# Gathering an MoE layer's tokens to partitions 32 to 95, with 28 of 64 experts on 64 slots

## What is computed

```python
scores = jax.nn.sigmoid(xf @ w_router)                  # 520 x 64
...
_, idx = lax.top_k(jnp.where(emask, biased, -jnp.inf), TOP_K)   # 8 of 64 experts per token
gates = w_sel / jnp.sum(w_sel, axis=-1, keepdims=True) * ROUTED_SCALE
...
hb = jax.nn.silu(xb @ w1_e[e]) * (xb @ w3_e[e])         # xb: the tokens of expert e
return (hb @ w2_e[e]) * g[:, None]
```

## Time and profile before

| | |
|---|---|
| median of three runs | 1209.22 us |
| the profiled execution's own time | 1210.91 us |
| its span, first to last instruction | 1209.1 us |
| PE / DVE / ACT / POOL, busy share of the span | 93% / 35% / 21% / 15% |
| mean granted TensorE clock | 0.98 of full speed |
| HBM read and written | 300.15 and 29.36 MB |
| gathers, and their issue on POOL | 64, about 0.98 us each |
| scatters, and their issue on POOL | 64, 1.01 to 1.13 us each |

### The profile page before, as it was taken

The page is one execution under the profiler, slowest core; times in us unless marked ns, Lnnn a source line. Parts: engine busy times, 40 slices in busy tenths (PEclk is TensorE's granted clock), DMA queues, the critical chain, the costliest instruction groups (busy, mean ns, idle before and its releaser), DMA issues.

```text
span 1209.1 us, 21090 instructions
## 1 busy us (share of the span) xinstructions
PE 1124.7 (93%) x8298; PEld 751.8 (62%) x8298; DVE 421.4 (35%) x1046; ACT 258.0 (21%) x566; POOL 176.2 (15%) x210
## 2 busy tenths in 40 slices
PE   7999997999988898999999999999999999999963
PEld 6888644877865687777655556555555555555410
DVE  0359998132058425741111212121121212112034
ACT  1101234022041125101122222222222222222200
POOL 3120050000000000112222222122221222212100
PEclk9999998999999999999999999999999999999978
DMA  9630404034047353358999999999999999999496
GB/s 331 239 140 1 157 13 174 1 140 157 1 140 272 146 211 146 125 186 307 350 385 386 374 386 389 387 388 389 387 381 381 384 387 390 385 383 373 152 379 256
DMA packets 66313, 319.16 MB, mean 264 GB/s; under 512 B 10311, under 2 KB 16671, under 8 KB 39629
## 3 DMA queue, kind: packets, MB, share of 16 engines
q1 hardware_dynamic: 51269, 278.60, 60.2%
q0 software_dynamic: 13568, 35.48, 8.6%
q10 hardware_dynamic: 1424, 4.35, 0.9%
HBM read 300.15 MB, written 29.36 MB: 273 GB/s over the span
## 4 chain that ended last, share of the span: by engine, by line
PE 67%; DVE 16%; DMA 13%; ACT 2%; issue 1%; SPq 1%; DVEq 0%; POOLq 0%
PE psum L755 60%; DMA arena<-in_w_e_dram 8%; DVE act_mem L1717 7%; PE psum L770 6%; DMA arena<-y_rows 3%; DVE mk_mem L1879 2%; DMA arena<-in_w_in_dram 1%; SPq L546 1%; DVE act_mem L1935 0%; ACT act_mem L1500 0%; DVE act_mem L2084 0%; DVE act_mem L1814 0%; ACT act_mem L1509 0%; DVE act_mem L1731 0%; DVE act_mem L2095 0%
## 5 line engine op out<-in xcount | busy, mean ns | idle before, releaser
L755 PE MATMUL psum<-arena,act_mem 128*32 128x128 f32 (+6 forms) x4800 | 509.1, 361 | 9.1 <-DMA arena<-in_w_e_dram 7.9
L755 PEld LDWEIGHTS psum<-arena,act_mem 128*32 128x32 f32 (+5 forms) x4800 | 260.6, 123 | 196.7 <-issue 107.5
L755 PE MATMUL psum<-act_mem,arena 128*128 128x260 f32 (+1 forms) x1728 | 357.7, 369 | 7.1 <-DMA arena<-in_w_o_dram 1.3
L755 PEld LDWEIGHTS psum<-act_mem,arena 128*128 128x128 f32 x1728 | 309.7, 195 | 52.6 <-DMA arena<-in_w_in_dram 2.4
L770 PE MATMUL psum<-ident,act_mem 96*128 96x96 f32 (+8 forms) x484 | 79.5, 296 | 16.5 <-DVE act_mem L1818 6.8
L678 POOL DMA_INDIRECT y_rows<-act_mem,idx_y x40 | 45.1, 1128 | 315.3 <-DVE idx_x L2116 169.8
L2128 DVE TENSOR_SCALAR act_mem<-psum,act_mem 96x512 f32<-96x512 f32 (+1 forms) x40 | 29.9, 747 | 157.7 <-PE psum L755 157.7
L1717 DVE SCALAR_TENSOR_TENSOR act_mem<-act_mem,wcb 128x511 f32<-128x511 f32 (+29 forms) x120 | 77.8, 735 | 0.0
L770 PEld LDWEIGHTS psum<-ident,act_mem 96*128 96x128 f32 (+8 forms) x484 | 59.1, 178 | 28.7 <-issue 12.3
L2125 DVE TENSOR_TENSOR act_mem<-act_mem,psum 128x192 f32<-128x192 f32 x35 | 12.4, 354 | 175.6 <-ACT act_mem L1573 175.6
L755 PEld LDWEIGHTS psum<-act_mem 128*96 128x96 bf16 (+4 forms) x379 | 27.0, 121 | 50.0 <-issue 49.3
(11 more groups left out here) (268 smaller groups left out, 717.6 us busy)
## 6 DMA issues: line engine op xcount, KB each, us to landing
arena<-in_w_e_dram SPq DMA_DIRECT2D x192, 1024.0 KB, 12.9
arena<-y_rows SPq DMA_DIRECT2D x8, 2048.0 KB, 23.9
arena<-in_w_in_dram SPq DMA_DIRECT2D x16, 512.0 KB, 18.1
arena<-in_cache_mem_k_dram SPq DMA_DIRECT2D x8, 1024.0 KB, 8.4
arena<-in_cache_mem_v_dram SPq DMA_DIRECT2D x8, 1024.0 KB, 11.8
arena<-in_w_v_dram SPq DMA_DIRECT2D x1, 4096.0 KB, 24.7
arena<-in_w_k_dram SPq DMA_DIRECT2D x1, 4096.0 KB, 13.8
arena<-in_w_out_dram SPq DMA_DIRECT2D x1, 4096.0 KB, 13.8
```

The source lines that it names most:

```text
L755: return pe.matmul(out, lhsT, rhs, start=first, stop=last)
```

## The change

There are 28 light positions instead of 24, in a period of 16. Apart from the big experts, tokens are gathered to partitions from 32 on: 32 to 95 for the first 64 tokens, 96 to 127 for what a heavy expert has beyond. These tokens beyond 64 have a gather and a scatter of their own (for big experts too), with semaphores `m_gm` and `m_sm` and row numbers `more_x` and `more_y`. PE transposes all 128 partitions for light and heavy experts alike, and ACT copies out the columns of the slots in use, in one instruction. The constants of POOL become 46 instead of 29.

```diff
+ROWS_AT = 32
-NB = 8
-LIGHT = (2, 5, 7)
-HEAVY = (0, 1, 3, 4, 6)
+NB = 16
+BIGS = 8
+LIGHT = (2, 4, 6, 9, 11, 13, 15)
+HEAVY = (0, 1, 3, 5, 7, 8, 10, 12, 14)
...
-SORT_CONSTS = 13 + 2 * NB
+SORT_CONSTS = 14 + 2 * NB
...
+def like(k, mod):
+
+    return [h for h in HEAVY if h % mod == k % mod]
+
+
+def halves_out(i, k, mod):
+
+    hs = like(k, mod)
+    return len(hs) * (i + k // NB) + sum(1 for h in hs if h <= k % NB)
...
-            number(slots_m.rearrange("p (e j) -> p e j", e=LANES), [[1, LANES], [LANES, MCAP // LANES]], 1)
+            number(slots_m[:, 0:LCAP].rearrange("p (e j) -> p e j", e=LANES), [[1, LANES], [LANES, LCAP // LANES]], 1)
+            number(slots_m[:, LCAP:MCAP].rearrange("p (e j) -> p e j", e=LANES), [[1, LANES], [LANES, MORE // LANES]], LCAP + 1)
...
-            def gather(n, b, s, cap=CAP):
+            def gather(n, b, s, cap=CAP, at=0, idx=idx_x):
                 gp.indirect_dma_start(
-                    out=xg[b][0:cap, :], out_offset=None, in_=x2_rows[:, :],
-                    in_offset=bass.IndirectOffsetOnAxis(ap=idx_x[0:cap, n:n + 1], axis=0),
+                    out=xg[b][at:at + cap, :], out_offset=None, in_=x2_rows[:, :],
+                    in_offset=bass.IndirectOffsetOnAxis(ap=idx[0:cap, n:n + 1], axis=0),
...
-                gather(n, n % 4, m_g[n % 4], LCAP if is_light(n) else CAP if is_big(e) else MCAP)
+                at = 0 if is_big(e) else ROWS_AT
+                gather(n, n % 4, m_g[n % 4], LCAP, at)
+                if not is_light(n):
+                    gather(n, n % 4, m_gm[n % 4], CAP - LCAP if is_big(e) else MORE, at + LCAP, more_x)
...
-                    scatter(n, n % 2, m_s[n % 2], CAP if is_big(e) else MCAP)
+                    scatter(n, n % 2, m_s[n % 2], LCAP)
+                    scatter(n, n % 2, m_sm[n % 2], CAP - LCAP if is_big(e) else MORE, LCAP, more_y)
...
-            def turn_few(n):
+            def turn_all(n):
                 for k in range(KC):
-                    last = turn(psum[:, 1, LCAP * k:LCAP * k + LCAP], xg[n % 4][0:LCAP, k:D:KC], LCAP)
+                    last = turn(psum[:, 1, P * k:P * k + P], xg[n % 4][:, k:D:KC])
                 return last
...
+            def b_step(e, k, i):
+                n = k % NB
+                pe.wait_ge(m_g[n % 4], 16 * (NB // 4 * i + (k // 4 + 1)))
+                if not is_light(n):
+                    pe.wait_ge(m_gm[n % 4], 16 * halves_out(i, k, 4))
                 if at_least(e, 1):
                     pe.wait_ge(m_xc, e)
...
+                (turn_rows if is_big(e) else turn_all)(n).then_inc(m_xt, 1)
...
-            def xc_most(b):
-                for h in range(2):
-                    last = act.activation(xgT[:, b, 4 * h:4 * h + 4, 0:MCAP],
-                                          psum[:, 1, 512 * h:512 * h + 4 * MCAP].rearrange("p (k s) -> p k s", k=4), ACT.Copy)
-                return last
+            def xc_part(b, cap):
+                return act.activation(xgT[:, b, :, 0:cap],
+                                      psum[:, 1, :].rearrange("p (k s) -> p k s", k=KC)[:, :, ROWS_AT:ROWS_AT + cap], ACT.Copy)
...
                 if sc is not None:
                     act.wait_ge(m_s[n % 2], sc)
+                    act.wait_ge(m_sm[n % 2], 16 * halves_out(i, k - 2, 2))
...
+                if split:
+                    dve.tensor_scalar(more_y[0:cap - LCAP, n:n + 1], picked[LCAP:cap, n, 0:1], FAR, None, ALU.add)
...
+                if split:
+                    dve.tensor_scalar(more_x[0:cap - LCAP, n:n + 1], more_y[0:cap - LCAP, n:n + 1], 3, None,
+                                      ALU.logical_shift_right)
```

More of the change, by code:

```diff
@@ L98, in is_big @@
 def is_big(e):
-    return isinstance(e, int) and e < NB and e % NB in HEAVY
+    return isinstance(e, int) and e < BIGS and e % NB in HEAVY
 def turned(e):
-    return lights(e) if isinstance(e, int) and e < NB else e - (len(HEAVY) - 1)
+    return e + 1 - sum(1 for h in HEAVY if h < BIGS and (not isinstance(e, int) or h <= e))
 def heavies(k):
     return k + 1 - lights(k)
+def like(k, mod):
[3 more added lines that the diff above has]
+    return len(hs) * (i + k // NB) + sum(1 for h in hs if h <= k % NB)
 def at_least(e, n):
@@ L232, in decoder_step @@
         idx_x = sb("idx_x", [P, NB], U32)
+        more_y = sb("more_y", [CAP - LCAP, NB], U32)
+        more_x = sb("more_x", [CAP - LCAP, NB], U32)
         over = sb("over", [P, 1], I32)
@@ L365, in decoder_step @@
         m_g = [sem(f"m_g{n}") for n in range(4)]
+        m_gm = [sem(f"m_gm{n}") for n in range(4)]
         m_xt = sem("m_xt")
@@ L377, in decoder_step @@
         m_s = [sem(f"m_s{n}") for n in range(2)]
+        m_sm = [sem(f"m_sm{n}") for n in range(2)]
         m_z = sem("m_z")
@@ L675, in scatter_halves, with scatter @@
                     bounds_check=last_half, oob_is_err=False).then_inc(s, 16)
-            def scatter(n, b, s, cap=CAP):
+            def scatter(n, b, s, cap=CAP, at=0, idx=idx_y):
                 gp.indirect_dma_start(
-                    out=y_rows[:, :], out_offset=bass.IndirectOffsetOnAxis(ap=idx_y[0:cap, n:n + 1], axis=0),
-                    in_=ys[0:cap, b, :], in_offset=None,
+                    out=y_rows[:, :], out_offset=bass.IndirectOffsetOnAxis(ap=idx[0:cap, n:n + 1], axis=0),
+                    in_=ys[at:at + cap, b, :], in_offset=None,
                     bounds_check=last_y, oob_is_err=False).then_inc(s, 16)
@@ L730, in _ @@
                 gp.wait_ge(m_s[1], 16 * (E // 2))
+                gp.wait_ge(m_gm[0], 16 * halves_out(E // NB - 1, NB - 4, 4))
+                for p in range(2):
+                    gp.wait_ge(m_sm[p], 16 * halves_out(E // NB - 1, NB - 2 + p, 2))
                 gp.sem_inc(f_sem["it"], 1)
@@ L1285, in _ @@
             wait_out(pe, "so2")
-            b_step(0, 0, 16)
+            b_step(0, 0, 0)
             wait_out(pe, "so3")
             c_step(0, 0, 48)
-            b_step(1, 1, 16)
+            b_step(1, 1, 0)
             wait_out(pe, "so4")
@@ L1615, in c_step, with y_step @@
                 (sl_few if is_light(n) else sl if is_big(e) else sl_most)(n % 2).then_inc(m_sl, 1)
-            def y_step(e, n, sc):
+            def y_step(e, k, i, sc):
+                n = k % NB
                 act.wait_ge(m_y, e + 1)
@@ L2137, in oh_step, with i_step @@
                     oh(n, e, slots if is_big(e) else slots_m, cap).then_inc(m_oh, 1)
-            def i_step(e, n, sc):
+            def i_step(e, k, i, sc):
+                n = k % NB
                 dve.wait_ge(m_ip, e + 1)
@@ L2142, in i_step @@
                     dve.wait_ge(m_s[n % 2], sc)
+                    if not is_light(n):
+                        dve.wait_ge(m_sm[n % 2], 16 * halves_out(i, k - NB, 2))
                 if is_light(n):
@@ L2168, in _ @@
             dve.tensor_copy(over[:, :], cmax).then_inc(s_over, 1)
-            i_step(0, 0, None)
+            i_step(0, 0, 0, None)
             oh_step(2, 2)
-            i_step(1, 1, None)
+            i_step(1, 1, 0, None)
             oh_step(3, 3)
@@ L2177, in _ @@
             dve.sem_inc(s_table, 1)
-            i_step(2, 2, None)
+            i_step(2, 2, 0, None)
             oh_step(4, 4)
             shared_sum(2)
-            i_step(3, 3, None)
+            i_step(3, 3, 0, None)
             oh_step(5, 5)
@@ L2188, in step @@
                 c_step(e, k % NB)
-                y_step(e - 1, (k - 1) % NB, sc)
+                y_step(e - 1, k - 1, i, sc)
                 if exists(e + 3):
-                    i_step(e + 3, (k + 3) % NB, si)
+                    i_step(e + 3, k + 3, i, si)
                 if exists(e + 5):
@@ L2198, in _ @@
             for k in range(1, NB + 1):
-                step(k, k, 0, None if k <= 2 else 16 * ((k - 1) // 2), None if k < 5 else 16 * ((k - 5) // 2 + 1))
+                step(k, k, 0, None if k <= 2 else 16 * ((k - 1) // 2), None if k < NB - 3 else 16 * ((k + 3 - NB) // 2 + 1))
             with dve.Fori(1, LAST) as i:
@@ L2202, in _ @@
                     step(NB * i + k, k, i, 16 * (NB // 2) * i + 16 * ((k - 1) // 2),
-                         16 * (NB // 2) * i + 16 * ((k - 5) // 2 + 1))
+                         16 * (NB // 2) * i + 16 * ((k + 3 - NB) // 2 + 1))
             for k in range(1, NB):
                 e = NB * LAST + k
-                step(e, k, LAST, 16 * ((e - 1) // 2), 16 * ((e - 5) // 2 + 1))
-            y_step(E - 1, NB - 1, 16 * ((E - 1) // 2))
+                step(e, k, LAST, 16 * ((e - 1) // 2), 16 * ((e + 3 - NB) // 2 + 1))
+            y_step(E - 1, NB - 1, LAST, 16 * ((E - 1) // 2))
             dve.wait_ge(s_over, 1)
```

35 lines of the change are left out of this document (13 added, 22 removed).

## The result

The changed kernel takes 1198.42 us (median of four runs, 1194.16 to 1199.92) where the kernel before, beside it, took 1209.76 (1207.23 to 1210.64): ratio 0.991, 95% interval 0.9888 to 0.9932. It is faster by 0.9%, 11 us, where 25 were forecast. The profiled run of it took 1194.16 us, the fastest of the four.

The account below looks back on a forecast made before the run. PE and DMA both bound the expert loop, weights arriving just in time. 1210.9 - 14.8 - 8.7 - 4 + 2 = 1185.4, less 1.7 to the median's scale: 1184 us, range 1177 to 1207.

Parts of the forecast that it names:

- the dip behind the gather: Expert loop: 16 DMA engines move 287 GB/s while the gather's packets run, 430 during the scatter's, 426 behind the gather.
- the rate above 395 GB/s: Sign of being right: the loop's DMA rate rises above 395 GB/s, from 385 before.
- mostly gone: Gathers to partitions 32 to 95: the dip mostly vanishes, PE sets the pace, 8.7 us of waits go.
- the dip stays: Rival, chance 0.13: the new placement doesn't help, PE's gain becomes waits for weights; 1209 us, between 1206 and 1213.
- Four more light experts, -14.8: PE in the expert loop: 28 light experts instead of 24, each 3.70 us shorter, save 14.8 us.
- Transposes, -4: PE in the expert loop: transposes of all 128 partitions run faster, 4 us less, bounds 0 and -8.
- For waits that survive ... I add 2 us: Expert loop: 2 us added for waits that remain with the DMA at 97% of PE's pace.
- part of the dip goes: Rival, chance 0.16: the dip goes only partly and DMA still sets the end; 1190 to 1205 us.
- Cost 0 here: POOL's queue: 72 more DMAs for tokens beyond 64 cost nothing, as the drain sets the landing and gets shorter.
- 3.0 us spare: Expert loop: margin between a gather's median landing, 9.1 us after issue, and PE's use of its rows.
- The rival's price: Late gathers, chance 0.07: PE waits on some 31; about 0.8 us each eats the gain, 1.3 us gives 1224.
- 8.7: PE's waits in the loop, 7.9 us for weights and 0.8 for gathered rows, expected to go: 8.7 us saved.

Follow-up runs that it names:

- the gather's part alone: Changed kernel with the old period (24 light experts, period of eight steps), gathers placed and split as changed: 1199.23 us, ratio 0.9923 to the kernel before.
- one loss cured: Two runs, each against the changed kernel: PE's loop written out, 1193.23 us; or POOL issuing gathers ahead of scatters, 1189.44 us.
- the clean run of it: Changed kernel with gathers ahead of scatters, PE's loop written out, and rows at partitions 0 to 63 and 64 to 95: 1219.59 us, ratio 1.0095.
- both cures: Changed kernel with POOL issuing gathers ahead of scatters and PE's loop written out, together: 1185.64 us, ratio 0.9803 to the kernel before.

## Why the prediction was right and wrong

- **What bounds the kernel** was read rightly: DMA and PE at nearly the same pace, the dip behind the gather as what held the DMA. With the gather's part alone the weights' wait (7.9 us) went to nothing. Of the signs named for being right, the rate above 395 GB/s didn't come with the change as it stands (391), but did with one loss cured (396 and 397) and with both (403).
- **The placement** was taken as "mostly gone" with the bound "the dip stays". Mostly gone is what happened. The bound was too narrow on the slow side: the rival had 1206 to 1213, and the clean run of it took 1219.6. It priced the old single gather and not the two that the change makes, which may be why.
- **Four more light experts, -14.8**: right. With no wait left, sixteen experts from 24 to 40 take 146.6 us in the kernel with both cures, as against 150.2 with the old period, 3.6 for one more light expert in sixteen.
- **Transposes, -4**: wrong. The row at 348 us comes from another stage. In the chain of the loop, like for like, eight transposes take 1.09 us after, and 1.02 (64 partitions) or 1.06 (96) before. The floor of eight experts, 75.21 us in the earlier trace rows, became 75.06 with 128 partitions throughout: about 1 us in the whole loop.
- **The step that failed** is "For waits that survive ... I add 2 us". The stretch took 515.1 us where the kernel without waits takes 501.5: 13.6 us of waits. Of these 7.7 are the stall at PE's jump, which no step of the sum had: the period's doubling was costed by what the experts do, not by the length of the loop's body. The other 5.9 are the late gathers; cured alone, with PE's loop written out, the order brings 508.9 to 501.5. The two overlap, so that a cure of one leaves a little more or less of the other.
- **Luck.** 1198 us lies in the band of "part of the dip goes", 1190 to 1205, and inside the stated range because that rival was in it. That is chance: 3 windows of the dip were left, not a part that set the pace, and the loss lay in PE's jump and POOL's order.
- **"Cost 0 here"** for the 72 DMAs failed by its reason that "the drain sets the landing, and it gets shorter". It did get shorter, 8.4 us in the median against 9.1, but by less than the 0.9 us by which PE came sooner and the 1.3 to 2.6 us by which the gathers were issued later. Of the 3.0 us spare, 0.2 to 1.5 are left at the median, and nothing for the slow ones, up to 9.8 us. The rival's price, all 31 heavy gathers late by 0.8 us, was too high: PE waits on some of them, by 0.3 to 1.5 us. The sum knew only none late or all late.

The rest of the sum holds: both cures together come out at 1185.6 us, 23.0 below the kernel before on the same chip. The forecast's terms with 1 for the transposes and nothing for surviving waits make 14.8 + 8.7 + 1 = 24.5.

## What to carry to other kernels

When a change lengthens a loop's body, count the instructions of each engine in it: a jump that was free with 1517 PE instructions cost 7.7 us with some 2900, over a third of it by the clock that fell behind it. The instruction queue in the profile tells whether a body stays at hand: it moved nothing round the short one. When an engine speeds up, price again every transfer that it used to wait behind something else for: an order of a queue that was harmless (gathers behind scatters, 0.8 us of wait) was worth 7 to 9 us once the other bound was gone. And here a gather of 64 rows belonged half on either side of partition 64; crossing it with 16 of 64 was not enough.

## What was not expected of the hardware

- Rows all above partition 64 cost as much as rows all below it (1217 and 1220 us against 1186), and 3 to 1 most of what 1 to 0 does (1221 and 1225 against 1199 without the cures).
- A jump back over some 2900 PE instructions stops PE for 4.8 to 5.3 us, and the granted clock is at 0.50 for some six microseconds after it. The instructions of the long body are fetched again on the second trip, 0.20 MB; those of the short one are not.
- Issued ahead of the scatter, a gather lands 0.8 to 1.0 us sooner after its issue in the median (7.4 against 8.2 and 8.4 us).
